# A gated-DeltaNet block on Trainium2: context blocks of both directions inverted in one pass on GpSimd, latent forward blocks on VectorE between the first merges, and the output projection in one stage

## The chip, the cores and the metric

The program runs on one core of a Trainium2 chip. A core has a matrix engine (TensorE, PE in the rows, its weight loads PEld), a vector engine (VectorE, DVE), a scalar engine (ScalarE, ACT), a general engine (GpSimd, POOL), a queue engine that issues DMAs (SyncE, SP), and 16 DMA engines. The metric is the device time of the whole program in microseconds (us); lower is better.

## The reference, cut to what matters

Two blocks run one after the other: a first block (bidirectional gated DeltaNet mixer, then a mixture of experts) and a second block of attention layers. All is float32. The change touches only the mixer's recurrence and its output projection. There are 8 heads of width 128, 256 context tokens and 512 latent tokens; each direction scans its context from a zero state and then its latent tokens from the state left.

```python
def chunk_gated_delta(q, k, v, g, beta, s0):
    a_low = jnp.where(strict, jnp.einsum('bhnid,bhnjd->bhnij', k_beta, k) * decay, 0.0)
    lmat = a_low + jnp.eye(CHUNK, dtype=f32)
    sol = lax.linalg.triangular_solve(lmat, rhs, left_side=True, lower=True, unit_diagonal=True)
    ...
def gdn_out(o, z, o_gain, w_out):
    o = o * lax.rsqrt(jnp.mean(o * o, axis=-1, keepdims=True) + RMS_EPS) * o_gain.astype(jnp.float32) * jax.nn.silu(zf)
    return o.reshape(B, T, H * DV).astype(z.dtype) @ w_out
```

## The kernel before, in words

The recurrence (`gdn_recurrence`, L919) works on token tiles of 128: two context tiles (CT) and four latent ones (LT). For each tile, each half of the heads (4 heads) and each direction there is one "piece", 24 in all: PE makes Gram products and sums of gates, ACT the decays (L1270), DVE the strictly triangular matrix A (`a_piece`, L1376) and, for latent tiles, the attention part (`att_piece`, L1383). SP stores both in DRAM (L991, L995); 4 buffers hold A and 3 hold the attention part, so DVE waits when a store is late.

The solve is by an explicit inverse. The 32x32 diagonal blocks are gathered back from DRAM with one block on each partition (L1004; runs of 128 bytes): 64 partitions for a direction's context, 128 for a direction's latent part. `BlockInverse` (L889) inverts all of them at once by 31 rows, numbered 0 to 30; each row is two dependent tensor operations, a product (L911) and a subtraction (L912), whose sizes grow from 31 to 256 elements and shrink again. `turn` (L916) then copies the transpose. SP writes inverse and transpose to DRAM (L1010, L1011) and reads them as block-diagonal tiles, with off-diagonal parts of A (L1031 to L1034).

Then come merges, numbered y = 4g + c, with g the step (a tile in each direction) and c the direction and half: `product32` (L1112) and `merge32` (L1121, L1124) on PE with `keep32` on ACT between them, DVE's `merged(y)` (`t_early` L1390, `w_full` L1393), then `product64` (L1133), `keep64`, `merge64` (L1143), `fill64` (L1288). `product32(y)` waits for `fill64(y-1)`. Merges 0 to 2 run alone ahead of the main loop, the others between the state updates. Merge 3 is ahead of step 0's solves.

Who inverts what: DVE the forward context blocks after all its pieces; GpSimd the backward context blocks, then the latent forward, then the latent backward ones. Each engine runs its instructions in the order written, and each waits only on semaphores.

`gdn_output` (L1471) normalises the output O (DVE L1520), transposes it on PE (L1544), multiplies by gain and SiLU(z) on DVE (L1526), and in a second block of code, `add_product` (L1556), multiplies by the output weights in float32 on PE (L1579: 64 products of 128x512, two records each), scales by a gate and adds the residual on DVE (L1597, L1599). Each block of code ends with all engines meeting. Elsewhere the kernel already multiplies with split operands: a high part rounded to float32r and a low remainder, three products in place of one (`split_product`, L117; `take_low`, L113).

## Time and profile before

| | us |
|---|---|
| median of 3 runs | 2742.77 (2737.44 to 2743.57) |
| the profiled execution's own time | 2743.18 |
| its span | 2741.4 |
| pieces (PE starts 400.2, DVE's last ends 466.9) | 67 |
| no PE work, DVE and POOL invert blocks | 467 to 516 |
| merges 0 to 3, then main loop | 516 to 737 |
| `gdn_output` with `add_product` | 739.0 to 817.2 |
| experts and second block after that | to the end |

| engine | busy us | share of the span |
|---|---|---|
| PE | 2335.7 | 85% |
| DVE | 1005.3 | 37% |
| ACT | 577.4 | 21% |
| POOL | 264.3 | 10% |

The engine shares are averages over stages that have different limits; the stage from 467 to 516 has none of PE's work in it. The chain of work that ended last, as the page prints it, covers only the last stage, so the chain through the recurrence was followed through the timelines of single engines.

### The profile page before, as it was taken

What the parts mean: (1) busy time and instruction counts of PE and PEld (TensorE: products, weight loads), DVE (VectorE), ACT (ScalarE), POOL (GpSimd) and SP (SyncE); (2) the same over time, 40 slices, a digit from 0 to 9 for tenths busy, and PEclk for the clock granted to TensorE, in tenths of its full rate; (3) what the DMA queues carried; (4) which work ended last, traced back from release to release, by engine and by line L of the source; (5) the groups of instructions that cost most, each with busy time, mean ns of one, the idle gap of its engine ahead of it and who ended that gap; (6) DMA issues with size and microseconds to landing.
All of it is one profiled execution on the core that took longest, in us unless ns stands there. A gap on an engine that the chain in (4) does not pass through costs nothing. (4 is left out here: it accounts for less than half of the span.)

```text
span 2741.4 us, 29858 instructions
## 1 busy us (share of the span) xinstructions
PE 2335.7 (85%) x11740; PEld 1512.8 (55%) x11740; DVE 1005.3 (37%) x1774; ACT 577.4 (21%) x1217; POOL 264.3 (10%) x355
## 2 busy tenths in 40 slices
PE   4999986389886888888888888875998989799998
PEld 2877666389835333333333333332775767687776
DVE  3677426335625101101010110104653554464443
ACT  4442213044401100000000000002222421223311
POOL 4233335800000000000000000000000000000000
PEclk8999988599996899999999999997998999899999
DMA  6124627144311799999999999994321022221030
GB/s 215 58 83 134 219 92 203 36 136 119 131 47 61 295 417 417 418 418 417 416 416 417 418 417 418 418 416 156 128 89 34 31 100 77 98 92 62 31 131 31
DMA packets 209191, 569.88 MB, mean 208 GB/s; under 512 B 62553, under 2 KB 97346, under 8 KB 175682
## 3 DMA queue, kind: packets, MB, share of 16 engines
q1 hardware_dynamic: 206296, 559.97, 53.8%
q0 software_dynamic: 2496, 8.40, 1.0%
q8 instruction: 68, 1.11, 0.2%
...
## 5 line engine op out<-in xcount | busy, mean ns | idle before, releaser
L1871 PE MATMUL ps_gate_up<-expert_ring_early,one_expert_columns 128*64 128x512 f32 x512 | 256.8, 660 | 87.7 <-DMA expert_ring_early<-in_moe_w_up_dram 73.9
L1871 PE MATMUL ps_gate_up<-expert_ring,one_expert_columns 128*64 128x512 f32 x512 | 235.3, 614 | 43.7 <-DMA expert_ring<-in_moe_w_up_dram 43.6
L1938 DVE TENSOR_TENSOR hidden_tokens<-silu_gate,ps_gate_up 64x512 f32<-64x512 f32 x64 | 42.4, 690 | 613.2 <-ACT silu_gate L1917 612.6
L1872 PE MATMUL ps_gate_up<-expert_ring_early,one_expert_columns 128*64 128x512 f32 x512 | 257.5, 661 | 0.0
L1872 PE MATMUL ps_gate_up<-expert_ring,one_expert_columns 128*64 128x512 f32 x512 | 236.0, 616 | 0.0
L1852 PE MATMUL ps_down<-expert_ring,hidden_columns 128*64 128x512 f32 x512 | 226.6, 595 | 0.0
L1851 PE MATMUL ps_down<-expert_ring,hidden_columns 128*64 128x512 f32 x512 | 226.6, 595 | 0.0
L1871 PEld LDWEIGHTS ps_gate_up<-expert_ring_early,one_expert_columns 128*64 128x64 f32 x512 | 74.8, 152 | 254.0 <-issue 254.0
L1871 PEld LDWEIGHTS ps_gate_up<-expert_ring,one_expert_columns 128*64 128x64 f32 x512 | 70.4, 141 | 190.5 <-issue 190.5
L1851 PEld LDWEIGHTS ps_down<-expert_ring,hidden_columns 128*64 128x64 f32 x512 | 67.5, 137 | 130.1 <-issue 127.9
L846 DVE SCALAR_TENSOR_TENSOR conv_out<-conv_in,tap_columns,conv_out 128x770 f32<-128x770 f32 (+1 forms) x96 | 122.3, 1274 | 3.4
L120 PE MATMUL even_bank<-stream_high,columns_high 128*128 128x512 f32 x256 | 108.8, 425 | 2.7 <-DVE columns_low L2440 2.7
L114 DVE TENSOR_TENSOR stream_low<-stream_raw,stream_high 128x2048 fp32r<-128x2048 f32 x48 | 110.0, 2292 | 1.6
L120 PE MATMUL odd_bank<-stream_high,columns_high 128*128 128x512 f32 x256 | 107.1, 418 | 2.8 <-DVE columns_low L2440 2.8
L110 DVE CAST stream_high<-stream_raw 128x2048 fp32r<-128x2048 f32 x48 | 58.6, 1221 | 137.3 <-PE out_bank L122 51.9
L120 PE MATMUL ps_lat<-u_columns_high,w_in_high 128*128 128x512 f32 x256 | 107.8, 421 | 0.0
L1917 ACT ACTIVATE silu_gate<-ps_gate_up 64x512 f32<-64x512 f32 x64 | 37.1, 588 | 330.5 <-PE ps_gate_up L1872 330.4
L611 POOL TENSOR_TENSOR w_in_low<-win_ring,w_in_high 128x1024 fp32r<-128x1024 f32 x32 | 84.3, 2634 | 217.9 <-ACT w_in_high L741 217.9
L121 PE MATMUL ps_lat<-u_columns_low,w_in_high 128*128 128x512 f32 x256 | 104.2, 407 | 0.0
L122 PE MATMUL ps_lat<-u_columns_high,w_in_low 128*128 128x512 f32 x256 | 104.1, 407 | 0.0
L121 PE MATMUL even_bank<-stream_low,columns_high 128*128 128x512 f32 x256 | 103.1, 403 | 0.0
L122 PE MATMUL even_bank<-stream_high,columns_low 128*128 128x512 f32 x256 | 103.0, 402 | 0.0
...
## 6 DMA issues: line engine op xcount, KB each, us to landing
...
```

The source lines that it names most:

```text
L110: return nc.vector.tensor_copy(high.bitcast(F32R), x)
L114: return nc.vector.tensor_tensor(low.bitcast(F32R), x, high, ALU.subtract)
L120: nc.tensor.matmul(out, sh, mh, start=start, stop=False)
L121: nc.tensor.matmul(out, sh, ml, start=False, stop=False)
L122: return nc.tensor.matmul(out, sl, mh, start=False, stop=stop)
L611: nc.gpsimd.tensor_tensor(wl[:, n % 2].bitcast(F32R), raw(n), wh[:, n % 2], ALU.subtract).then_inc(low, 1)
L846: ins = nc.vector.scalar_tensor_tensor(out=cv[:, n % 2, a:b], in0=pad[:, n % 2, a + j:b + j], scalar=tap(j), in1=cv[:, n % 2, a:b], op0=AL ...
L1851: mm(psD[LO, e], hT[:, f], dn[n % RING][:, r, 0:COLS], start=(f == 0), stop=(f == FC - 1))
L1852: last = mm(psD[HI, e], hT[:, f], dn[n % RING][:, r, COLS:D], start=(f == 0), stop=(f == FC - 1))
L1871: mm(psA[LO, c], xe[:, e, k], gu[s0][:, j, cols], start=(k == 0), stop=(k == KC - 1))
L1872: last = mm(psA[HI, c], xe[:, e, k], gu[s1][:, j, cols], start=(k == 0), stop=(k == KC - 1))
L1938: nc.vector.tensor_tensor(hid[HI, c % 2], sg[HI, c % 2], psA[HI, c], ALU.mult).then_inc(hidden, 1)
```

## The change

- The context gathers of both directions move from SP to ACT's queue, after the tenth decay. The backward direction's blocks land in `El[0]`, a buffer of the latent inversion, and GpSimd turns them (a transposing copy) into the upper half of `Ec`. A backward triangle turned is a forward one, so one pass of 31 rows on 128 partitions, on GpSimd, inverts both directions; the stores swap inverse and transpose for the backward half.
- GpSimd then inverts the latent backward blocks only. DVE inverts the latent forward blocks after its pieces, with merges 0, 1 and 2 after rows 14, 23 and 30.
- SP stores all 24 pieces without a break; the context gathers and the first loads of k and v no longer stand between the stores of the 8 context and the 16 latent pieces. Those loads now follow the first inputs.
- `gdn_output` and `add_product` become one block of code. The weights are split in four pieces by ACT (high) and GpSimd (low), the columns by ACT and DVE, and the product is 192 float32r products instead of 64 float32 ones. The residual is loaded after the last transpose.

```diff
-                def blocks(u, d, upto):
+                def blocks(d):
                     for i in range(AB):
-                        sp.wait_ge(a_stored[i], 16 * len(range(i, upto, AB)))
-                    E, t0, t1 = (Ec, 0, CT) if u == 0 else (El[d], CT, NT)
-                    n = (t1 - t0) * HEADS
+                        sp.wait_ge(a_stored[i], 16 * len(range(i, len(PIECES), AB)))
+                    if d == 0:
+                        sp.wait_ge(ctx_turned, 1)
+                    n = LT * HEADS
                     for b in range(BLOCKS):
-                        p0 = (d * UNIT_P[0] if u == 0 else 0) + b * n
-                        sp.dma_start(E[p0:p0 + n], A_dram[d][span(b), t0:t1, :, span(b)].rearrange("j t h i -> (t h) j i")).then_inc(e_loaded[u, d], 16)
+                        src = A_dram[d][span(b), CT:NT, :, span(b)].rearrange("j t h i -> (t h) j i")
+                        sp.dma_start(El[d][b * n:(b + 1) * n], src).then_inc(e_loaded[1, d], 16)
...
-                    E, X = (Ec, Xc) if u == 0 else (El[d], Xl[d])
-                    part = slice(d * UNIT_P[0], (d + 1) * UNIT_P[0]) if u == 0 else slice(0, P)
-                    sp.wait_ge(inverted[u, d], 1)
-                    sp.dma_start(W_dram[u][d], X[part].rearrange("p a b -> p (a b)")).then_inc(scattered[u, d], 16)
-                    sp.dma_start(T_dram[u][d], E[part].rearrange("p a b -> p (a b)")).then_inc(scattered[u, d], 16)
+                    if u == 0:
+                        part = slice(d * UNIT_P[0], (d + 1) * UNIT_P[0])
+                        W, T = (Xc[part], Ec[part]) if d == 0 else (Ec[part], Xc[part])
+                        sp.wait_ge(inverted[0, 0], 1)
+                    else:
+                        W, T = Xl[d][:, :, :], El[d][:, :, :]
+                        sp.wait_ge(inverted[1, d], 1)
...
-                store(range(0, LAT0))
+                store(range(0, len(PIECES)))
                 for d in DIRS:
-                    blocks(0, d, LAT0)
+                    blocks(d)
+                for d in DIRS:
+                    scatter(0, d)
+                for d in DIRS:
+                    inputs(0, d)
                 for d in DIRS:
                     load_v(0, d)
                     load_k(0, d)
-                store(range(LAT0, len(PIECES)))
-                for d in DIRS:
-                    blocks(1, d, len(PIECES))
-                scatter(0, 0)
-                inputs(0, 0)
-                scatter(0, 1)
-                inputs(0, 1)
...
-                for i in range(len(PIECES)):
+                for i in range(LAT0 + 2):
+                    decay(i)
+                for i in range(AB):
+                    act.wait_ge(a_stored[i], 16 * len(range(i, LAT0, AB)))
+                for d, E, p0 in ((0, Ec, 0), (1, El[0], UNIT_P[0])):
+                    for b in range(BLOCKS):
+                        src = A_dram[d][span(b), 0:CT, :, span(b)].rearrange("j t h i -> (t h) j i")
+                        act.dma_start(E[p0 + b * CT * HEADS:p0 + (b + 1) * CT * HEADS], src).then_inc(e_loaded[0, d], 16)
+                for i in range(LAT0 + 2, len(PIECES)):
...
-                h1 = slice(UNIT_P[0], 2 * UNIT_P[0])
-                for u, d, inv in ((0, 1, BlockInverse(Ec[h1], Xc[h1], tmp[1][h1], True)),
-                                  (1, 0, BlockInverse(El[0][:, :, :], Xl[0][:, :, :], tmp[1][:, :], False)),
-                                  (1, 1, BlockInverse(El[1][:, :, :], Xl[1][:, :, :], tmp[1][:, :], True))):
-                    inv.clear(nc.gpsimd, seq)
-                    if u == 0:
-                        seq(nc.gpsimd.memset(O, 0.0))
-                    pool.wait_ge(e_loaded[u, d], 16 * BLOCKS)
-                    for j in range(ROWS):
-                        inv.row(nc.gpsimd, seq, j)
-                    inv.turn(nc.gpsimd).then_inc(inverted[u, d], 1)
-                    pool.wait_ge(inverted[u, d], 1)
+                back = slice(UNIT_P[0], 2 * UNIT_P[0])
+                ctx_inv = BlockInverse(Ec[:, :, :], Xc[:, :, :], tmp[1][:, :], False)
+                lat_inv = BlockInverse(El[1][:, :, :], Xl[1][:, :, :], tmp[1][:, :], True)
+                ctx_inv.clear(nc.gpsimd, seq)
+                seq(nc.gpsimd.memset(O, 0.0))
+                lat_inv.clear(nc.gpsimd, seq)
+                for d in DIRS:
+                    pool.wait_ge(e_loaded[0, d], 16 * BLOCKS)
+                nc.gpsimd.tensor_copy(Ec[back], El[0][back].rearrange("p a b -> p b a")).then_inc(ctx_turned, 1)
+                pool.wait_ge(ctx_turned, 1)
+                for j in range(ROWS):
+                    ctx_inv.row(nc.gpsimd, seq, j)
+                ctx_inv.turn(nc.gpsimd).then_inc(inverted[0, 0], 1)
+                pool.wait_ge(inverted[0, 0], 1)
+                pool.wait_ge(e_loaded[1, 1], 16 * BLOCKS)
+                for j in range(ROWS):
+                    lat_inv.row(nc.gpsimd, seq, j)
+                lat_inv.turn(nc.gpsimd).then_inc(inverted[1, 1], 1)
...
-                h0 = slice(0, UNIT_P[0])
-                ctx_inv = BlockInverse(Ec[h0], Xc[h0], tmp[0][h0], False)
+                lat_inv = BlockInverse(El[0][:, :, :], Xl[0][:, :, :], tmp[0][:, :], False)
+                MERGED_AFTER = {14: 0, 23: 1, 30: 2}
...
-                ctx_inv.clear(nc.vector, seq)
+                lat_inv.clear(nc.vector, seq)
                 for i in range(len(PIECES)):
                     piece(i)
-                dve.wait_ge(e_loaded[0, 0], 16 * BLOCKS)
+                dve.wait_ge(e_loaded[1, 0], 16 * BLOCKS)
                 for j in range(ROWS):
-                    ctx_inv.row(nc.vector, seq, j)
-                ctx_inv.turn(nc.vector).then_inc(inverted[0, 0], 1)
-                merged(0)
-                merged(1)
-                merged(2)
+                    lat_inv.row(nc.vector, seq, j)
+                    if j in MERGED_AFTER:
+                        merged(MERGED_AFTER[j])
+                lat_inv.turn(nc.vector).then_inc(inverted[1, 0], 1)
...
+                for i in range(HALVES):
+                    c = i // 2 * COLS
+                    sp.dma_start(raw[:, i], w[:, i % 2 * HK:(i % 2 + 1) * HK, c:c + COLS]).then_inc(w_loaded[i], 16)
+                    if i == 0:
+                        sp.dma_start(szT[:, :, :], z_dram).then_inc(z_loaded, 16)
+                sp.wait_ge(turned, HEADS)
+                sp.dma_start(h[:, :, :], residual).then_inc(h_loaded, 16)
...
+                def weights_high(i):
+                    act.wait_ge(w_loaded[i], 16)
+                    nc.scalar.activation(wh[:, i].bitcast(F32R), raw[:, i], ACT.Copy).then_inc(w_high, 1)
...
+                weights_high(0)
+                weights_high(1)
+                keep_row(0, "gate_mix")
+                for k in range(HEADS):
+                    act.wait_ge(kept, k + 1)
+                    nc.scalar.activation(sh[:, k].bitcast(F32R), szT[:, k], ACT.Copy).then_inc(s_high, 1)
+                weights_high(2)
+                weights_high(3)
+                keep_row(1, "gate_ffn")
...
+                for i in range(HALVES):
+                    pool.wait_ge(w_high, i + 1)
+                    nc.gpsimd.tensor_tensor(wl[:, i].bitcast(F32R), raw[:, i], wh[:, i], ALU.subtract).then_inc(w_low, 1)
...
-                for h in range(HEADS):
-                    dve.wait_ge(turned, h + 1)
-
-                    nc.vector.scalar_tensor_tensor(out=szT[:, h], in0=ps[:, h % 2], scalar=gain, in1=szT[:, h],
-                                                   op0=ALU.mult, op1=ALU.mult).then_inc(kept, 1)
+                for k in range(HEADS + 1):
+                    if k < HEADS:
+                        dve.wait_ge(turned, k + 1)
+
+                        nc.vector.scalar_tensor_tensor(out=szT[:, k], in0=ps[:, k % 2], scalar=gain, in1=szT[:, k],
+                                                       op0=ALU.mult, op1=ALU.mult).then_inc(kept, 1)
+                    if k:
+                        dve.wait_ge(s_high, k)
+                        take_low(nc, sl[:, k - 1], szT[:, k - 1], sh[:, k - 1]).then_inc(s_low, 1)
+                dve.wait_ge(h_loaded, 16)
+                dve.wait_ge(row_kept, 1)
...
-        add_product(nc, "gdn_w_out", per, szT, wt, gate=per["gate_mix"],
-                    residual=dram["x"].rearrange("b (t p) d -> p (b t) d", p=P))
+                pe.wait_ge(row_kept, 1)
+                rows(1, 5)
+                for n in range(2 * LT):
+                    i, t = n // LT, n % LT
+                    if i:
+                        pe.wait_ge(taken, t + 1)
+                    for k in range(KC):
+                        if t == 0 and k % HK == 0:
+                            pe.wait_ge(w_low, 2 * i + k // HK + 1)
+                        if n == 0:
+                            pe.wait_ge(s_low, k + 1)
+                        half = 2 * i + k // HK
+                        last = split_product(nc, psD[:, t], [x[:, k, t * P:(t + 1) * P] for x in (sh, sl)],
+                                             [x[:, half, k % HK] for x in (wh, wl)], k == 0, k == KC - 1)
+                    last.then_inc(done, 1)
...
-            recycle(nc)
-            gdn_output(nc, dram, per, O, z_dram)
+        recycle(nc)
+        gdn_output(nc, dram, per, O, z_dram)
```

**ACT** in the row of decays, just where the latent pieces begin. Before:

```order
L1270 ACTIVATE decay<-gdn_bank,token_scalars 128x128 [waits a_ready,rowsums]
L1270 ACTIVATE decay<-gdn_bank,token_scalars 128x128 x3
L1270 ACTIVATE decay<-gdn_bank,token_scalars 128x128 [waits a_ready,rowsums]
L1270 ACTIVATE decay<-gdn_bank,token_scalars 128x128 x3
L1270 ACTIVATE decay<-gdn_bank,token_scalars 128x128 [waits a_ready,rowsums]
```

Now:

```order
L1272 ACTIVATE decay<-gdn_bank,token_scalars 128x128 [waits a_ready,rowsums]
L1272 ACTIVATE decay<-gdn_bank,token_scalars 128x128 x3
L1314 DMA blocks_ctx<-a_turned 16x32x32 [waits a_stored2,a_stored3,a_stored1,a_stored0]
L1314 DMA blocks_ctx<-a_turned 16x32x32 x3
L1314 DMA blocks_lat<-a_turned 16x32x32 x4
L1272 ACTIVATE decay<-gdn_bank,token_scalars 128x128 [waits att_ready,a_ready,rowsums]
L1272 ACTIVATE decay<-gdn_bank,token_scalars 128x128 x3
```

Eight gathers, with a wait for the stores of the first 8 pieces, now stand between two decays.

**DVE** at the end of the inversion and the first merges. Before, all 31 rows on the context blocks stand ahead of the turn and of merge 0:

```order
L911 TENSOR_TENSOR row_update<-blocks_ctx,inverse_ctx 64x31 [waits row_chain0]
L912 TENSOR_TENSOR inverse_ctx<-inverse_ctx,row_update 64x31 [waits row_chain0]
L916 COPY blocks_ctx<-inverse_ctx 64x1024 [waits row_chain0]
L1390 TENSOR_TENSOR t_early<-t_diagonal,gdn_bank 64x256 [waits x1_done]
L1393 TENSOR_TENSOR w_full<-w_diagonal,gdn_bank 128x512 [waits x2_done]
```

Now, around merge 0 (row 14 is the one on 255 elements):

```order
L911 TENSOR_TENSOR row_update<-blocks_lat,inverse_lat 128x255 [waits row_chain0]
L912 TENSOR_TENSOR inverse_lat<-inverse_lat,row_update 128x15x17 [waits row_chain0]
L1406 TENSOR_TENSOR t_early<-t_diagonal,gdn_bank 64x256 [waits x1_done,row_chain0]
L1409 TENSOR_TENSOR w_full<-w_diagonal,gdn_bank 128x512 [waits x2_done]
L911 TENSOR_TENSOR row_update<-blocks_lat,inverse_lat 128x256
L912 TENSOR_TENSOR inverse_lat<-inverse_lat,row_update 128x16x16 [waits row_chain0]
```

The same two instructions of a merge stand again after the row of 192 elements (row 23) and after the last. DVE's rows are now on the latent blocks and on both sides of a merge.

**SP** where the inverse of the context leaves. Before, each direction is stored and read by itself:

```order
L1010 DMA w_blocks<-inverse_ctx 64x1024 [waits inverted00]
L1011 DMA t_blocks<-blocks_ctx 64x1024
L1031 DMA t_diagonal<-t_blocks 32x8x32 [waits diagonals_zeroed,scattered00]
L1031 DMA t_diagonal<-t_blocks 32x8x32 x3
L1031 DMA w_diagonal<-w_blocks 32x8x32 x4
L1033 DMA a_off_0<-a_turned 32x8x32 x2
```

Now:

```order
L1015 DMA w_blocks<-inverse_ctx 64x1024 [waits inverted00]
L1016 DMA t_blocks<-blocks_ctx 64x1024
L1015 DMA w_blocks<-blocks_ctx 64x1024 [waits inverted00]
L1016 DMA t_blocks<-inverse_ctx 64x1024
L1036 DMA t_diagonal<-t_blocks 32x8x32 [waits diagonals_zeroed,scattered00]
```

Both directions wait for the same semaphore, GpSimd's, and both stores stand ahead of the first read.

## Rows read from the trace of the kernel before

**Rows 1.** Windows: us, busy (x) of PE, PEld, DVE, ACT, POOL, PEclk, DMA share, GB/s.

```profile
423.00:431.00 8.00, 8.00 (x75) 8.00 (x73) 5.87 (x19) 3.84 (x15) 0.00 (x0) 1.00 1.02 119
446.00:466.00 20.00, 17.57 (x158) 17.38 (x156) 15.03 (x46) 10.03 (x36) 17.65 (x31) 0.98 0.59 221
467.00:516.00 49.00, 0.00 (x0) 0.00 (x0) 35.12 (x62) 0.00 (x0) 40.09 (x70) 0.50 0.35 56
```

**Rows 2.** Timelines of ACT, SP, POOL: context gathers (start us, us, engine line op).

```profile
422.87 1.15 ACT L1270 ACTIVATE decay<-gdn_bank,token_scalars 128x128 f32<-128x128 f32 x4 [0.20 <-PE gdn_bank L1103]
...
422.87 4.02 SPq L1004 DMA_DIRECT2D blocks_ctx<-a_turned  x8
...
431.01 0.25 POOL L911 TENSOR_TENSOR row_update<-blocks_ctx,inverse_ctx 64x31 f32<-64x31 f32 x1 [20.40 <-DMA blocks_ctx<-a_turned]
...
468.04 1.89 POOL L916 COPY blocks_ctx<-inverse_ctx 64x1024 f32<-64x1024 f32 x1
```

**Rows 3.** Timelines of DVE: its last piece, then the forward context inversion.

```profile
466.17 0.68 DVE L1383 TENSOR_TENSOR att_piece<-gdn_bank,decay 128x512 f32<-128x512 f32 x1
...
480.04 0.56 DVE L911 TENSOR_TENSOR row_update<-blocks_ctx,inverse_ctx 64x256 f32<-64x256 f32 x1
...
492.63 0.67 DVE L911 TENSOR_TENSOR row_update<-blocks_ctx,inverse_ctx 64x175 f32<-64x175 f32 x1
...
502.75 1.46 DVE L916 COPY blocks_ctx<-inverse_ctx 64x1024 f32<-64x1024 f32 x1
```

**Rows 4.** Timelines of SP and PE: inverse stored, then the first merge product.

```profile
504.24 0.53 SPq L1010 DMA_DIRECT2D w_blocks<-inverse_ctx  x1
...
516.24 2.07 PE L1112 MATMUL gdn_bank<-t_diagonal,a_off 128*128 128x128 f32 x8 [52.67 <-DMA a_off<-a_turned]
```

**Rows 5.** Timeline of DVE: merges 0, 2 and 3 ahead of the main loop.

```profile
520.14 0.41 DVE L1390 TENSOR_TENSOR t_early<-t_diagonal,gdn_bank 64x256 f32<-64x256 f32 x1 [15.93 <-PE gdn_bank L1121]
...
522.15 0.69 DVE L1393 TENSOR_TENSOR w_full<-w_diagonal,gdn_bank 128x512 f32<-128x512 f32 x1 [1.59 <-PE gdn_bank L1124]
...
538.20 0.42 DVE L1390 TENSOR_TENSOR t_early<-t_diagonal,gdn_bank 64x256 f32<-64x256 f32 x1 [6.34 <-PE gdn_bank L1121]
...
547.22 0.42 DVE L1390 TENSOR_TENSOR t_early<-t_diagonal,gdn_bank 64x256 f32<-64x256 f32 x1 [6.33 <-PE gdn_bank L1121]
```

**Rows 6.** Timelines of POOL and DVE: rows side by side, and the copy.

```profile
474.83 0.38 POOL L911 TENSOR_TENSOR row_update<-blocks_lat,inverse_lat 128x31 f32<-128x31 f32 x1 [3.67 <-DMA blocks_lat<-a_turned]
...
501.34 0.60 POOL L911 TENSOR_TENSOR row_update<-blocks_lat,inverse_lat 128x231 f32<-128x231 f32 x1
...
501.37 0.64 DVE L911 TENSOR_TENSOR row_update<-blocks_ctx,inverse_ctx 64x31 f32<-64x31 f32 x1
...
514.01 1.91 POOL L916 COPY blocks_lat<-inverse_lat 128x1024 f32<-128x1024 f32 x1
```

**Rows 7.** Timelines of DVE and SP: the stall among pieces, the latent gathers.

```profile
438.37 0.69 DVE L1383 TENSOR_TENSOR att_piece<-gdn_bank,decay 128x512 f32<-128x512 f32 x1 [8.39 <-DMA attention<-att_piece]
...
468.95 5.99 SPq L1004 DMA_DIRECT2D blocks_lat<-a_turned  x8
```

**Rows 8.** Timelines of DVE and PE in the output stage.

```profile
745.58 4.63 DVE L1520 TENSOR_TENSOR residual<-residual,o_ss 128x1024 f32<-128x1024 f32 x4
...
751.49 6.02 DVE L1526 SCALAR_TENSOR_TENSOR silu_z_again<-o_ps,vector_columns,silu_z_again 128x512 f32<-128x512 f32 x8 [1.28 <-PE o_ps L1544]
...
758.88 56.87 PE L1579 MATMUL gdn_w_out_ps<-gdn_w_out_pieces,silu_z_again 128*128 128x512 f32 x128 [2.15 <-PEq L1488]
...
816.50 0.69 DVE L1599 TENSOR_TENSOR residual<-residual,gdn_w_out_tmp 128x512 f32<-128x512 f32 x1
```

**Rows 9.** Timeline of PE in the second block, and the page's group of L611.

```profile
2152.78 0.40 PE L120 MATMUL even_bank<-stream_high,columns_high 128*128 128x512 f32 x1
...
2154.16 0.39 PE L120 MATMUL even_bank<-stream_high,columns_high 128*128 128x512 f32 x1
...
L611 POOL TENSOR_TENSOR w_in_low<-win_ring,w_in_high 128x1024 fp32r<-128x1024 f32 x32 | 84.3, 2634 | 217.9 <-ACT w_in_high L741 217.9
```

102 lines of the change are left out of this document (37 added, 65 removed).

## The prediction

> **What bounds the kernel now.** I read the windows first. From 467 to 516 us PE does nothing, its granted clock is 0.50, and DVE and GpSimd are busy for 35 and 40 of the 49 us [rows 1]. Next, DVE's timeline: its last piece ends at 466.9, the 31 inversion rows of the forward context blocks follow without a gap, the turn ends at 504.2 [rows 3]. SP then stores the inverse, and PE's first merge product comes at 516.24, after 52.67 us of idleness [rows 4]. So the stage's end is set by DVE inverting after its pieces, though GpSimd had inverted the other direction by 469.9 [rows 2]. Then merges 0 to 3 run one after the other, 9.0 us each: DVE's `t_early` stands at 520.14, 538.20 and 547.22 for merges 0, 2 and 3 [rows 5]. The output stage is bound by PE: 56.87 us of float32 products [rows 8].
>
> **The new chain into the merges.** I place everything on the clock of the old trace.
>
> *Gathers.* ACT ends its tenth decay at 424.0; eight issues took SP 4.0 us, so they end at 428.0; the last landed 4.1 us after its issue (426.9 to 431.0) [rows 2], so 432.1. But now SP's stores run beside them. Stores alone keep the DMA engines at 0.59, gathers alone at 1.02 [rows 1]. If the shares simply add, the gathers get 0.41 of the engines and their 8.1 us become 19.8, 11.7 us more. The latent gathers speak against that: twice the bytes (256 blocks against 128) were issued in 6.0 us [rows 7], so the context's need at most some 3 us of the engines' capacity, and 3/0.41 is 7.3, no delay. I take 2 us (0 to 11.7), nearer to the second row since it is of the same kind of transfer: 434.1. The Trainium skill (DMA: Bandwidth & Descriptors, Queues, rings and completion order) says that a DMA engine takes turns between queues packet by packet; by it neither queue starves, which would put the delay in the lower half, and no row here shows two queues at once.
>
> *One pass for both directions.* First the turning copy, 1.9 us like GpSimd's copy of the same size [rows 2]: 436.0. The pass has 128 partitions. On 64 it took 37.0 us (431.01 to 468.04) [rows 2], on 128, beside DVE's rows, 39.2 (474.83 to 514.01) [rows 6]; so partitions cost nothing, and most of the new pass runs beside the pieces. I take 37.8: 473.8, with the copy 475.7. The store began at 504.24 before [rows 4]; it is 28.5 us earlier. From store to first product 12.0 us passed [rows 4]; the second direction's store lies in the wait for the first to land. So the first product is at 487.7, merge 0's `t_early` 3.9 us on, at 491.6, and its `w_full` ends 6.6 us on, at 494.3 [rows 4, 5].
>
> *The pieces.* DVE waited 8.39 us for an attention store that stood in SP's queue behind gathers and the loads of k and v [rows 7]. These are gone from there; eight issues on ACT delay two decays by some 2 us, which PE's lead hides but for under 1. Pieces end near 459. Latent gathers and landing took 8.0 us (466.85 to 474.83) [rows 3, 6], so DVE's rows start at 467. This gain is worth nothing: rows 0 to 14 took 13.3 us, to 480.04 [rows 3], and even at 20 us, beside GpSimd, end before 491.6. If the stall stays, its 8 us only just use up this slack.
>
> *Rows between merges.* This is what is late next. At the end of the old pass the two engines' rows run in step: GpSimd's operation on 231 elements starts at 501.34 and takes 0.60, DVE's on 31 elements starts at 501.37 and takes 0.64 [rows 6]. A small DVE row costs what GpSimd's large one costs. In the new kernel GpSimd is in its latent pass from 475.7 to 516.8 all the while. Rows 15 to 23 took 12.6 us (480.04 to 492.63) [rows 3] with GpSimd in rows of like size; they start at 494.3, after merge 0, and end at 506.9. PE would have had merge 1 ready at 500.6 (491.6 + 9.0), so it waits 6.3. Merge 1 is 1.1 us of DVE (0.41 + 0.69) [rows 5]: 508.0. Rows 24 to 30 took 10.1 (492.63 to 502.75) [rows 3] beside GpSimd's largest rows; now it is in its last ones and its copy. I take 8.6 (4 to 10.1): merge 2's `t_early` at 516.6 instead of 538.20, 21.6 earlier. PE's other products of merge 2 are done by then, so the wait of 1.59 behind `t_early` [rows 5] goes: merge 3 is 23.1 us earlier, at 524.1. DVE's turn (1.5 us) ends near 519, GpSimd's pass at 516.8; both latent inverses are there before the main loop begins and are first used in its third step. The first k and v loads move behind the first inputs and have over 20 us. The loop itself is unchanged.
>
> **The output stage.** Now DVE's four normalising operations (4.63 us) are followed by eight of scaling (6.02), and PE starts its product at 758.88, 1.4 us after them, a block boundary that goes [rows 8]. Added ahead of the product: eight `take_low` on DVE at 0.69, as for the same size in the last row, 5.5 us [rows 8]. GpSimd subtracts four pieces of 128x2048; half that size takes 2.63 [rows 9], so 5.3 each. By the row in step [rows 6], a DVE operation with both inputs in SBUF waits until GpSimd's ends: the first subtraction then holds up normalising by 5 us (0 to 5.3), the second the first `take_low` by 1.5 (0 to 5.3, part of it lies in a wait for ACT). The Trainium skill (SBUF — State Buffer, Who interferes with whom) says just this: a VectorE instruction with two SBUF inputs and a GpSimd one that reads SBUF exclude each other for a whole instruction, and PE never waits; the trace agrees where it has such a pair, 0.64 for 31 elements. By that rule the stage gains next to nothing; were there no such lock it would gain 6.5 us more. ACT's four weight copies have no row; between nothing and 2.9 (twice DVE's 1.46 for half the elements [rows 3]), I take 2 and call them hidden under loads and DVE. The loads are the same 6 MB, which before had landed when PE began. The second gate row on PE, at most 4.1 us (twice 2.07 for half the products [rows 4]), lies under DVE's last columns. So the product starts 5.5 + 5 + 1.5 - 1.4 = 10.6 us later. Three float32r products take 0.69 us (six starts in 1.38) [rows 9], 192 take 44.2, and I add 1 for the low clock at the start: 45.2 against 56.87, 11.7 less. Net 1.1 us gained (7.6 gained to 3 lost).
>
> **Sum.** 2743.2 (the profiled execution's own time) - 23.1 - 1.1 = 2719.0. The median of the runs is 0.4 below that execution; I stay at 2719. What follows the stage (experts, second block) starts by its own barriers and shifts as a whole: the expert loads are issued after this stage, not at a fixed time.
>
> **Rivals.**
> 1. *No lock, or a lighter one.* DVE's rows at their own pace never hold a merge: merge 3's `t_early` at 491.6 + 27.1 = 518.7, 28.5 gained, and the output stage 7.6: 2707 (2713 if only the rows are free). For it: merges with an input in PSUM took 0.41 and 0.69 throughout, with GpSimd at work or not. Against it: the rows in step [rows 6]. 0.14.
> 2. *Gathers slowed by stores*, the full 11.7 us: GpSimd's pass, the first product and the rows behind it all move by 9.7: 2729. For it the shares that add to over 1 [rows 1], against it the faster latent gathers [rows 7]. 0.15.
> 3. *Slower: the lock goes to GpSimd twice for each DVE operation.* In the old pass DVE got in after each one. If it gets in after every second, the 16 rows behind merge 0 pay 32 times 0.65, 20.8 us, row 14 ends some 3.4 us after merge 0 is ready, and merge 3 is 1.1 us later than before; with the output's 3 lost: 2747. It decides from the point where a DVE row operation beside GpSimd takes over some 1.3 us. Against it: 0.64 in the trace. 0.04.
> 4. *The gain is given back later*, in the expert stage, which waits for its loads; it would need loads issued at a fixed time, and they are not. 2742. 0.04.
>
> **How the numbers follow.** The forecast has 0.58, with its own range 2713 to 2725 (rows 24 to 30 at either end, gathers at 0 to 4). The remaining 0.05 are mixtures of rivals 1 and 2 with it, inside the range. From 2707 to 2731 (rival 2 with rows 24 to 30 at 10.1) about 0.9 lie; the unknown costs need that width. A difference under 0.2%, 5.5 us, cannot be told from no change. Faster: forecast, rivals 1 and 2 and mixtures, 0.93 with what such a sum leaves out; same 0.03 (most of rival 4); slower 0.04.
>
> **What would show it.** Right: GpSimd's first row near 436 and one pass of 37 to 39 us; PE's first merge product near 488 instead of 516; DVE idle ahead of merge 0 and PE waiting for DVE ahead of merges 1 and 2; merge 3's `t_early` 23 us earlier; the main loop (547 to 737) as long as before; `take_low` or normalising operations of 5 us beside GpSimd; the output product 45 us, starting 30 us into its stage. Wrong: context gathers landing after 438, DVE rows of 128x31 at 0.2 us beside GpSimd, or a main loop that waits for a latent inverse.

## The result

Over the first comparison the changed kernel took 2703.49 us (median of 4 runs, 2697.10 to 2709.14) against 2743.17 us (4 runs, 2737.44 to 2743.85): a ratio of 0.9859 with a 95% interval of 0.9832 to 0.9886. That is 39.7 us less, where 24.2 had been predicted, and 3.5 us under the low end of the range. The direction and the mechanism in the recurrence came out as forecast, the size did not. Two more comparisons of the same pair, made among the experiments below, gave 0.9891 (0.9863 to 0.9919) and 0.9883 (0.9864 to 0.9903). The medians of all runs, 52 of the kernel before and 15 of the changed one, are 2738.0 and 2705.7, 32.3 us apart. So some 7 us of the first difference did not repeat.

In the changed kernel L911 and L912 are still the rows of an inversion, L916 the turn; L1406 is `t_early` (L1390 before), L1570 the normalising (L1520 before) and L120 to L122 are the three products of a split product. Timelines have the start in us, the duration in us, engine, line and operation, tiles written and read, and in brackets the idle time before and what ended it.

The windows of the changed kernel (PE, PEld, DVE, ACT, POOL busy; then PE's granted clock, share of the DMA engines, GB/s), against [rows 1]:

```profile
466.00:485.00 19.00, 0.31 (x1) 0.32 (x2) 14.60 (x29) 0.00 (x0) 16.43 (x34) 0.50 0.53 95
485.00:521.00 36.00, 25.05 (x137) 21.61 (x137) 23.59 (x40) 4.66 (x10) 24.47 (x41) 0.50 0.31 82
```

PE now idles for 19 us where it had idled for 49. The chain that ends this gap, on GpSimd, SP and PE (against [rows 2, 4]):

```profile
431.04 1.99 POOL L1367 COPY blocks_ctx<-blocks_lat 64x1024 f32<-64x1024 f32 x1 [20.15 <-DMA blocks_lat<-a_turned]
470.19 1.89 POOL L916 COPY blocks_ctx<-inverse_ctx 128x1024 f32<-128x1024 f32 x1
472.11 0.53 SPq L1015 DMA_DIRECT2D w_blocks<-inverse_ctx  x1
484.69 2.08 PE L1114 MATMUL gdn_bank<-t_diagonal,a_off 128*128 128x128 f32 x8 [30.64 <-DMA a_off<-a_turned]
504.71 1.11 PE L1135 MATMUL gdn_bank<-t_early,a_off 64*64 64x64 f32 x8 [5.12 <-DVE t_early L1406]
```

The turning copy starts at 431.04 (434.1 was predicted), the one pass for both directions takes 37.0 us, and the first product comes at 484.69 (487.7). The last line is the new wait that was predicted: PE stands 5.12 us for merge 1's `t_early`, because DVE is still at its rows. DVE itself, against [rows 5]:

```profile
488.67 0.41 DVE L1406 TENSOR_TENSOR t_early<-t_diagonal,gdn_bank 64x256 f32<-64x256 f32 x1 [7.10 <-PE gdn_bank L1123]
493.34 0.78 DVE L912 TENSOR_TENSOR inverse_lat<-inverse_lat,row_update 128x255 f32<-128x255 f32 x1
504.25 0.41 DVE L1406 TENSOR_TENSOR t_early<-t_diagonal,gdn_bank 64x256 f32<-64x256 f32 x1
510.70 1.96 DVE L912 TENSOR_TENSOR inverse_lat<-inverse_lat,row_update 128x31 f32<-128x31 f32 x1
520.88 0.42 DVE L1406 TENSOR_TENSOR t_early<-t_diagonal,gdn_bank 64x256 f32<-64x256 f32 x1 [5.39 <-PE gdn_bank L1123]
```

Merge 0 comes at 488.67, after 7.10 us in which DVE did nothing, merge 1 at 504.25, 15.6 later instead of 9.0, merge 3 at 520.88, 26.3 us earlier than in [rows 5]. The line at 510.70 shows a row operation of 31 elements that takes 1.96 us: GpSimd's turn of 1.93 us starts at 510.66. The prediction had named a row of 31 elements at 0.2 us beside GpSimd as a sign against it, and there is one: the subtraction at 465.85 takes 0.19. It begins together with GpSimd's operation on 135 elements, and this one then takes 0.51 instead of the 0.42 of the same operation at 436.30. So it is not always DVE that waits.

The output stage, DVE, GpSimd and PE (against [rows 8]):

```profile
716.94 8.93 DVE L1570 TENSOR_TENSOR residual<-residual,o_ss 128x1024 f32<-128x1024 f32 x4
728.60 2.21 DVE L114 TENSOR_TENSOR o_columns_low<-silu_z_again,o_columns_high 128x512 fp32r<-128x512 f32 x1
737.70 1.47 DVE L114 TENSOR_TENSOR o_columns_low<-silu_z_again,o_columns_high 128x512 fp32r<-128x512 f32 x2
718.40 5.25 POOL L1560 TENSOR_TENSOR gdn_w_out_low<-gdn_w_out_raw,gdn_w_out_high 128x2048 fp32r<-128x2048 f32 x1 [7.47 <-ACT gdn_w_out_high L1531]
736.21 2.61 PE L1599 MATMUL ps_row<-identity_and_ones,mod_columns 128*128 128x128 f32 x16
738.58 0.47 PE L120 MATMUL gdn_w_out_ps<-gdn_w_out_high,o_columns_high 128*128 128x512 f32 x1
```

Normalising takes 8.93 instead of 4.63 and the first `take_low` 2.21 instead of 0.69, both beside a GpSimd subtraction. PE's product starts at 738.58, while DVE's last low parts are still being made, and ahead of it stands the second gate row. DVE's last addition ends at 783.83, and with it the stage's work.

### The profile page after: what moved, and what is told of

Its sections match the earlier page's. It is cut to its first block and busy times, and to the rows that moved or that the text cites. A ratio compares the mean times of both kernels' runs of the same rounds, so it can differ in the third digit from the quotient of the medians.

```text
span 2699.5 us, 29938 instructions
## 1 busy us (share of the span) xinstructions
PE 2307.3 (85%) x11804; PEld 1514.6 (56%) x11804; DVE 1019.7 (38%) x1782; ACT 589.6 (22%) x1229; POOL 249.5 (9%) x295
## 5 line engine op out<-in xcount | busy, mean ns | idle before, releaser
L1897 PE MATMUL ps_gate_up<-expert_ring_early,one_expert_columns 128*64 128x512 f32 x512 | 252.0, 650 | 87.6 <-DMA expert_ring_early<-in_moe_w_up_dram 73.8
L1898 PE MATMUL ps_gate_up<-expert_ring_early,one_expert_columns 128*64 128x512 f32 x512 | 252.8, 651 | 0.0
L120 PE MATMUL even_bank<-stream_high,columns_high 128*128 128x512 f32 x256 | 107.7, 421 | 2.8 <-DVE columns_low L2466 2.8
L120 PE MATMUL odd_bank<-stream_high,columns_high 128*128 128x512 f32 x256 | 107.0, 418 | 2.8 <-DVE columns_low L2466 2.8
L120 PE MATMUL ps_lat<-u_columns_high,w_in_high 128*128 128x512 f32 x256 | 108.0, 422 | 0.0
L611 POOL TENSOR_TENSOR w_in_low<-win_ring,w_in_high 128x1024 fp32r<-128x1024 f32 x32 | 84.3, 2636 | 217.9 <-ACT w_in_high L741 217.9
L122 PE MATMUL ps_lat<-u_columns_high,w_in_low 128*128 128x512 f32 x256 | 104.1, 407 | 0.0
L122 PE MATMUL even_bank<-stream_high,columns_low 128*128 128x512 f32 x256 | 102.6, 401 | 0.0
## 6 DMA issues: line engine op xcount, KB each, us to landing
expert_ring<-in_moe_w_up_dram SPq DMA_DIRECT2D x32, 2048.0 KB, 24.2
```

The source lines that it names most:

```text
L120: nc.tensor.matmul(out, sh, mh, start=start, stop=False)
L122: return nc.tensor.matmul(out, sl, mh, start=False, stop=stop)
L611: nc.gpsimd.tensor_tensor(wl[:, n % 2].bitcast(F32R), raw(n), wh[:, n % 2], ALU.subtract).then_inc(low, 1)
L1897: mm(psA[LO, c], xe[:, e, k], gu[s0][:, j, cols], start=(k == 0), stop=(k == KC - 1))
L1898: last = mm(psA[HI, c], xe[:, e, k], gu[s1][:, j, cols], start=(k == 0), stop=(k == KC - 1))
```

## Where the time went, stage by stage

One cut serves for all the profiles: A, from the first decay on ACT behind 400 us to merge 3's `t_early`; B, from there to the end of the last state update; C, the output stage, to the issue of the router's weights; D, the router stage, to the clearing of the experts' total; E, the experts, from the first accumulation to the last gated output; F, from there to the last residual addition of the second block. "Rise" is how long behind the start of B the granted clock of PE goes from 0.50 to 1.00. All worked out from starts in the timelines, in us.

```
                    A     rise    B      C      D      E      F
before            141.9   13.7  190.2   81.0   90.5   863.0  838.9
before, again     140.8    8.6  188.2   81.3   90.5   860.3  838.6
output only       140.2    9.3  188.1   76.6   86.8   860.0  837.6
recurrence only   116.4    8.7  188.0   80.6   89.5   860.2  834.5
changed           116.6    8.5  187.9   76.3   86.5   860.1  837.7
changed, second   115.9    9.2  188.3   76.5   86.5   860.0  837.6
changed, third    114.7   14.2  190.7   77.8   90.4   863.0  839.0
```

The first profiled execution of each kernel, "before" and "changed", differ by 41.9 us at their last operation. A is 25.3 of these, C 4.7 and the start of the first decay 1.0; B, D, E and F bring 10.4 more (the rest is rounding and a step between D and E), and a third profile of the very same changed kernel (last line) has given all of these back. So they can't be put down to the change; in B and D they go with the stretches in which the clock stands at 1.2 or 2.4 GHz (below), for E and F no row shows why. In D one thing stays open. In the four profiles with the old output stage D was 89.5 to 90.5; in the twelve with a new one, those of the experiments below among them, it was 86.5 to 86.8 seven times and 90.2 to 90.5 five times. The new output stage may make the short D possible, which on average would be worth some 2 us; so few profiles don't show it. The mean of A is 141.0 in three profiles without the new recurrence and 115.9 in the four with it, C is 81.0 in three with the old output stage and 76.8 in four with the new one: 25.1 and 4.2, 29.3 us of the change that the stages show.

## The experiments

**Each part alone, and the whole again.** One kernel has the new recurrence with the old `gdn_output` and `add_product`, the other the old recurrence with the new `gdn_output`; the functions are taken over word for word.

> The changed kernel once more, beside the kernel before and the two kernels that do one part each. Theory (the gain is 28.6 us in the recurrence, 4.7 in the output stage, 3.1 in the router stage and the rest, 5.5, in expert and second-block stages by chance of the run): the median comes to 2743 - 36.4 = 2706.5, within the spread of 2697 to 2709, and the stages up to the first expert matmul repeat to 1 us (merge 3's t_early 320 to 321 after 200 us, that is near 520.9; end of the recurrence near 708.5; first expert matmul near 876), while the 3.2 us between the first and the last expert do not repeat. Rival (the change does something to the expert stage): the expert stage is again 3 us shorter than in the kernel before and the median is again near 2703.

> The recurrence part of the change alone; output stage as before. Theory: merge 3's t_early at 520.9, the main loop (t_early of merge 3 to the end of the recurrence) 2.3 us shorter than before because the granted clock of PE rises some 6 us earlier in it, the recurrence ends 28.6 us earlier; then the float32 product and a router stage whose 64 small matmuls take 12.5 us as before. Total 2743 - 28.6 = 2714.5. Rival (router and experts gain from the recurrence part): total 2703 + 4.7 = 2708, and router matmuls near 10.1 us.

> The output stage of the change alone; recurrence as before. Theory: stage 4.7 us shorter (73.5 against 78.2), then the 64 router matmuls 10.1 us instead of 12.5 and the transposes ahead of them 0.8 us shorter, because the granted clock of PE, higher after the float32r product, falls later; total 2743 - 4.7 - 3.1 = 2735. Rival (the clock in the router stage is chance, or comes from the recurrence): router matmuls 12.5 us, total 2738.5.

Measured, beside 17 runs of before with median 2737.47: the whole 2705.89 (6 runs), the recurrence alone 2710.74 (6 runs, ratio 0.9904, 0.9879 to 0.9930), the output stage alone 2727.26 (12 runs, 0.9965, 0.9945 to 0.9986). The whole repeats in A to C (its starts are 3.5 to 4 us later, since its first decay is 4.1 later), and its median is the forecast one. The 3 us of the expert stage, which had been called chance of the changed kernel, repeated too (E 860.0). The totals expected were counted from 2743, while the kernel before took 2737.47 here; so the differences are what compares. The recurrence alone, with A and B of the changed kernel, takes 26.7 us less where 28.6 were expected. The output stage alone takes 10.2 less where 7.8 were expected; its profile has C 4.4 and D 3.7 shorter than the first of before. The theory that the output part alone decides the router stage's 86.5 us fitted these profiles and fell later: with the same output stage D took 90.4 in the changed kernel's third profile and in the kernel with moved rows. The two parts add up to 36.9 us where the whole has 31.6, which such medians leave open (5.5 us from run to run).

So the kernel before was profiled again:

> The kernel before once more, for a second profile. Theory (part of the 41.9 us between the two profiled executions is chance of the first profile of before): the expert stage, from its first to its last accumulation, takes 858.8 us as in every other kernel and not 861.8; the loop from merge 3's t_early to the end of the recurrence takes 187 us, not 189.05, where the granted clock rises earlier; the router stage (from its weight load to the first memset of the experts) stays at 89.5 to 90.5 us, against 86.5 in kernels with the new output stage. Rival (before's stages really are longer): 861.8, 189.0 and 90.5 repeat.

One run, 2740.20 us. In the table above (whose cuts B and E are 1.1 and 1.2 us longer than those of the expectations) B fell to 188.2 with a rise at 8.6, E to 860.3, and D stayed at 90.5: what the first profile of before had more in B and E did not repeat, as the theory says. It is one profile.

**Is it GpSimd that makes DVE's rows long?** GpSimd begins its latent pass only behind DVE's:

```diff
                 pool.wait_ge(e_loaded[1, 1], 16 * BLOCKS)
+                pool.wait_ge(inverted[1, 0], 1)
                 for j in range(ROWS):
```

> As the changed kernel, but GpSimd begins its latent pass only when DVE has ended its own (one wait more; the pass then runs from about 508 to 547 beside the main loop, whose third step uses it). Theory (a DVE operation with both inputs in SBUF waits for GpSimd's): without GpSimd rows 0 to 14 take under 10 us instead of 16.3, rows 15 to 23 under 8 instead of 13.0 and rows 24 to 30 under 5, so merge 1 follows merge 0 after 9.0 us instead of 15.6, PE's wait of 5.12 ahead of merge 1 goes, and merge 3's t_early stands at 515.8 instead of 520.9; total 5 us less than the changed kernel, unless the loop's DVE operations now wait for GpSimd or its third step for the inverse (it would be 0 to 8 more). Rival (the rows cost that much by themselves): rows 15 to 23 take 12 to 13 us again and merge 3 stays at 520.9.

DVE in this kernel, for the rows beside those shown above:

```profile
491.70 0.41 DVE L1407 TENSOR_TENSOR t_early<-t_diagonal,gdn_bank 64x256 f32<-64x256 f32 x1 [9.03 <-PE gdn_bank L1123]
495.61 0.42 DVE L912 TENSOR_TENSOR inverse_lat<-inverse_lat,row_update 128x255 f32<-128x255 f32 x1
502.07 0.41 DVE L1407 TENSOR_TENSOR t_early<-t_diagonal,gdn_bank 64x256 f32<-64x256 f32 x1
518.71 0.42 DVE L1407 TENSOR_TENSOR t_early<-t_diagonal,gdn_bank 64x256 f32<-64x256 f32 x1 [5.39 <-PE gdn_bank L1123]
```

The same subtraction on 128x255 takes 0.42 without GpSimd and 0.78 beside it; rows 15 to 23 take 7.8 us instead of 13.0, merge 1 follows merge 0 after 10.4 instead of 15.6 (9.0 had been expected, but the rows start only behind merge 0's 2.5 us on DVE) and merge 3 after 27.0 instead of 32.2. The lock (a DVE operation with both inputs in SBUF waits until GpSimd's ends) is real and costs 5.2 us here. The Trainium skill (SBUF — State Buffer, Who interferes with whom) says that such a pair of instructions excludes each other for the whole instruction. The changed kernel's trace agrees: 1.96 us for 31 elements beside a copy of 1.93. GpSimd's pass, now beside the main loop, ends at 552.5 and holds nothing up: B is 190.1 with a late rise (14.4), as in the third profile of the changed kernel. The first 15 rows took 13.9, not under 10: until 475.2 GpSimd was still in its context pass. The median is 2699.61 (4 runs; ratio 0.9848, 0.9813 to 0.9883); the 5 us less than the changed kernel are seen in the stage, the ratios' intervals overlap.

**Rows where DVE idles.** If the rows are long, they can be put elsewhere:

```diff
-                MERGED_AFTER = {14: 0, 23: 1, 30: 2}
+                MERGED_AFTER = {18: 0, 22: 1, 28: 2}
```

> As the changed kernel, but DVE takes merges 0, 1 and 2 after rows 18, 22 and 28 instead of 14, 23 and 30. Theory (beside GpSimd a row costs 1.45 us, and rows 15 to 23 hold up merge 1 by 6.6 us while DVE stood idle for 7.1 us ahead of merge 0): rows 15 to 18 go into that idle time (5.8 us), rows 19 to 22 take 5.8, merge 1's t_early comes 9.0 us behind merge 0's and merge 3's 27.1 behind it instead of 32.2; total 5.1 us less than the changed kernel, if the clock in the main loop rises at the same place. Rival (later rows hold merge 2, or the loop waits for the inverse that DVE now ends later): merge 3 gains under 2 us, or the third step starts later by what merge 3 gained.

```profile
496.34 0.41 DVE L1406 TENSOR_TENSOR t_early<-t_diagonal,gdn_bank 64x256 f32<-64x256 f32 x1 [1.05 <-PE gdn_bank L1123]
505.37 0.41 DVE L1406 TENSOR_TENSOR t_early<-t_diagonal,gdn_bank 64x256 f32<-64x256 f32 x1 [0.25 <-PE gdn_bank L1123]
523.35 0.42 DVE L1406 TENSOR_TENSOR t_early<-t_diagonal,gdn_bank 64x256 f32<-64x256 f32 x1 [2.34 <-PE gdn_bank L1123]
```

The idle time of 7.10 ahead of merge 0 is down to 1.05, merge 1 follows after 9.03, merge 3 after 27.01: 5.2 us less between merge 0 and merge 3, as expected, with GpSimd at work all the while. The median is 2698.99 (5 runs; 0.9854, 0.9833 to 0.9874).

**The gathers, and the first loads of k and v.** Two kernels: one issues the context gathers on SP behind the stores of the context pieces, the other puts the four first loads of k and v back to where they stood. The edit of the second:

```diff
-                store(range(0, len(PIECES)))
+                store(range(0, LAT0))
+                for d in DIRS:
+                    load_v(0, d)
+                    load_k(0, d)
+                store(range(LAT0, len(PIECES)))
...
-                for d in DIRS:
-                    load_v(0, d)
-                    load_k(0, d)
```

> As the changed kernel, but the eight context gathers are issued by SP, in its one queue, behind the stores of the context pieces, instead of by ACT. Theory (the gathers were never slowed, and only the slack of the pieces hangs on the queue): GpSimd's turning copy starts where it did, 26.7 us behind the first decay (plus or minus 1); the pieces end some 4 to 8 us later, because stores of attention pieces stand behind the gathers, DVE's first row comes that much later and still ends row 14 ahead of merge 0; merges and total stay within 1 us of the changed kernel. Rival (ACT's own queue is what keeps the gathers fast, beside the stores): the turning copy starts 2 us or more later and all merges move with it.

> As the changed kernel, but the four first loads of k and v go out between the stores of the context pieces and those of the latent pieces on SP, where they stood before the change. Theory (those loads, not the gathers, made the wait of 8.39 us, and the pieces have slack): DVE waits again 6 to 8.4 us for a store of an attention piece, the last piece ends some 61 us behind the first decay instead of 53, DVE's rows start 8 us later, row 14 ends at about merge 0's readiness (2 us before to 2 after); the turning copy stays within 1 us, merge 3 comes 0 to 2 us later and the total within 2 us of the changed kernel. Rival (the queue does not matter, the pieces are faster for another reason): the last piece again ends 52 to 53 us behind the first decay.

With the gathers on SP nothing is later: the turning copy starts 25.6 us behind the first decay (26.7 in the changed kernel), the pieces end 52.2 behind it (53.0), and the median is 2700.89 (4 runs; 0.9864, 0.9843 to 0.9885). The expected 4 to 8 us of stall did not come, so the move of the gathers to ACT's queue bought nothing.

With the loads early the forecast came out in one half. The pieces end at 59.8, which costs nothing by itself, row 14 being done 4.6 us ahead of merge 0. But the turning copy starts 31.3 us behind the first decay, 5.3 later than the mean of 26.0 in four profiles with the new recurrence, and A is 121.2 instead of 115.9. The issues, with KB each and median us from issue to landing, first with the loads early (424 to 440), then in the changed kernel (421 to 440); below them the issuing of the last four gathers (ACTq) and what came of it:

```profile
v_tile<-v_tokens SPq DMA_DIRECT2D x2, 512.0 KB, 5.7
blocks_ctx<-a_turned ACTq DMA_DIRECT2D x4, 64.0 KB, 10.2
blocks_lat<-a_turned ACTq DMA_DIRECT2D x4, 64.0 KB, 4.9
...
432.19 4.57 ACTq L1315 DMA_DIRECT2D blocks_lat<-a_turned  x4
436.88 2.18 ACT L1273 ACTIVATE decay<-gdn_bank,token_scalars 128x128 f32<-128x128 f32 x8 [10.08 <-issue]
438.11 1.13 DVE L1393 SCALAR_TENSOR_TENSOR a_piece<-gdn_bank,token_scalars,decay 128x128 f32<-128x128 f32 x4 [9.21 <-issue]
```

```profile
blocks_ctx<-a_turned ACTq DMA_DIRECT2D x4, 64.0 KB, 3.1
blocks_lat<-a_turned ACTq DMA_DIRECT2D x4, 64.0 KB, 4.4
...
424.13 3.15 ACTq L1314 DMA_DIRECT2D blocks_lat<-a_turned  x4
```

So the gathers are slowed from another queue, but by the 2 MB of k and v, beside which the DMA engines' share is 1.00 from 424 to 436, and not by the stores. The first four land after 10.2 us instead of 3.1. The last four, for which the turning copy waits, land after 4.9 instead of 4.4, but are issued late: the eight issues take ACT 11.0 us (425.80 to 436.76) instead of 5.2. DVE's wait of 9.21 us is not the one that was expected either. It does not stand ahead of an attention part, for a store, but ahead of an A, for a decay, and ACT makes this decay only when its issues are out. The median is 2711.69 (4 runs; 0.9916, 0.9892 to 0.9939), not within 2 us of the changed kernel.

**The loads alone, in the kernel before.** The same four loads moved behind the first inputs, and nothing else:

> The kernel before with one edit: the four first loads of k and v go out on SP behind the first inputs, as in the changed kernel, instead of between the stores of the context and of the latent pieces. Theory (these 2 MB, not the gathers, made DVE's wait of 8.39 us, and before the change DVE's rows follow its pieces without a gap): the last piece ends 52 to 53 us behind the first decay instead of 60 to 61.6, all of the chain behind it moves, merge 3's t_early comes 132 to 134 us behind the first decay instead of 140.8 to 141.9, and the total is 7.5 us less than before (6 to 9). Rival (the gathers alone keep the queue blocked, or the gathers' landing sets the end through GpSimd): under 2 us.

```profile
456.22 0.68 DVE L1383 TENSOR_TENSOR att_piece<-gdn_bank,decay 128x512 f32<-128x512 f32 x1
538.52 0.42 DVE L1390 TENSOR_TENSOR t_early<-t_diagonal,gdn_bank 64x256 f32<-64x256 f32 x1 [6.34 <-PE gdn_bank L1121]
```

Here the wait of 8.39 us ahead of an attention part is down to 1.33, with the gathers still on SP, so it was the loads'. The last piece ends 51.0 us behind the first decay and merge 3 stands at 132.7, 8.3 us earlier than the mean of before; median 2727.34 (5 runs; 0.9948, 0.9935 to 0.9962), 11.8 less than before and more than the 6 to 9 expected. A third of what the recurrence part gained could be had with this move alone. The other 16.8 us of A are left for the single pass on GpSimd and the new place of the rows, which no run separates. That the total gained 11.8 and A only 8.3 is not explained by a stage.

**The output stage.** First the low parts of the first two weight quarters on DVE:

```diff
-                for i in range(HALVES):
+                for i in range(2, HALVES):
                     pool.wait_ge(w_high, i + 1)
...
+                dve.wait_ge(w_high, 1)
+                take_low(nc, wl[:, 0], raw[:, 0], wh[:, 0]).then_inc(w_low, 1)
...
+                    if k == 4:
+                        dve.wait_ge(w_high, 2)
+                        take_low(nc, wl[:, 1], raw[:, 1], wh[:, 1]).then_inc(w_low, 1)
```

> As the changed kernel, but DVE itself takes the low parts of the first two quarters of the output weights (one between normalising and scaling, one behind the fourth column), GpSimd only those of the last two. Theory (a GpSimd subtraction excludes DVE operations with two SBUF inputs): the four normalising operations take 4.63 us again instead of 8.93, the first take_low of the columns 0.67 instead of 2.21, and DVE pays 2 times 2.3 us for the two quarters, one of them under a wait of 1.3; the product starts 26 us into the stage instead of 28.2, gain 2 us (0 to 3). Rival (the 4.3 us were something else, as cold SBUF reads or the loads of the weights): normalising takes 8.9 us again and the product starts 3 us later than in the changed kernel.

```profile
719.50 4.63 DVE L1570 TENSOR_TENSOR residual<-residual,o_ss 128x1024 f32<-128x1024 f32 x4
730.40 0.69 DVE L114 TENSOR_TENSOR o_columns_low<-silu_z_again,o_columns_high 128x512 fp32r<-128x512 f32 x1 [2.75 <-ACT o_columns_high L1548]
727.02 1.91 ACT L1531 ACTIVATE gdn_w_out_high<-gdn_w_out_raw 128x2048 fp32r<-128x2048 f32 x1 [5.73 <-DMA gdn_w_out_raw<-in_gdn_w_out_dram]
```

Normalising is back at 4.63, so the 4.3 us were GpSimd's. The product starts 30.7 us behind the last state update, later than the changed kernel's 29.8 and not 2 us earlier as expected. The stage gained nothing (C 77.6, as the changed kernel's third profile with 77.8; median 2707.32, 6 runs): ACT stands 5.73 us for the load of the second quarter, with the columns queued behind it, and DVE waits 2.75 for them. Under the lock this wait for a load had been hidden. The next kernel takes these waits and the second gate row out of the way of the product: DVE takes the second quarter's low part behind the columns, ACT converts that quarter behind the fifth column, PE makes the second gate row ahead of the transposes. Cut to the order:

```diff
-                weights_high(0)
-                weights_high(1)
                 keep_row(0, "gate_mix")
+                weights_high(0)
                 for k in range(HEADS):
...
+                    if k == 4:
+                        weights_high(1)
...
+                dve.wait_ge(w_high, 1)
+                take_low(nc, wl[:, 0], raw[:, 0], wh[:, 0]).then_inc(w_low, 1)
...
+                dve.wait_ge(w_high, 2)
+                take_low(nc, wl[:, 1], raw[:, 1], wh[:, 1]).then_inc(w_low, 1)
...
                 rows(0, 2)
+                pe.wait_ge(row_kept, 1)
+                rows(1, 5)
                 pe.wait_ge(normed, LT)
```

> As the changed kernel, with another order in the output stage: DVE takes the low parts of the first two weight quarters (one behind normalising, one behind the eighth column), GpSimd those of the last two; ACT converts the second quarter behind the fifth column instead of ahead of the first, where it waited 5.4 to 5.7 us for its load; PE makes the second gate row before the transposes instead of ahead of the product. Theory (normalising held 4.3 us by GpSimd, then ACT's columns held by the second quarter's load, then 2.6 to 3.6 us of the gate row on PE): normalising takes 4.63, no take_low waits 2.75 for ACT, and the product starts 24 to 25.5 us into the stage instead of 28.2; the stage is 3 to 4 us shorter. Rival (the first product waits for loads or for the second quarter's low part anyway): it starts by 25 but stands at its fifth step for 2 us or more, and the stage gains under 1.5.

> Both edits: merges 0, 1, 2 after rows 18, 22, 28, and the new order of the output stage. Theory: they lie in different stages and add up, 5.1 us and 3 to 4 us less than the changed kernel, that is a total of some 2696 to 2698 beside 2705.6 for the changed kernel and 2738.9 for the one before (medians of all their runs). Rival: one of the two is off the path, total 2700 or more.

```profile
735.97 0.78 PE L120 MATMUL gdn_w_out_ps<-gdn_w_out_high,o_columns_high 128*128 128x512 f32 x1
741.90 0.50 PE L120 MATMUL gdn_w_out_ps<-gdn_w_out_high,o_columns_high 128*128 128x512 f32 x1 [1.64 <-DVE gdn_w_out_low L114]
```

These are PE's first and fifth step in the kernel with the new order alone. The product starts 22.4 us behind the last state update instead of 29.8, begins slowly (0.78 for its first matmul instead of 0.47) and waits 1.64 at its fifth step, in which the rival had its part; C is 72.1, 4.2 to 5.7 less than in the profiles of the changed kernel, where 3 to 4 had been expected. In the total this gain is not shown: the median of this kernel, 2704.24 (6 runs, 0.9889, 0.9867 to 0.9911), can't be told from the changed kernel's. With the rows moved too: 2697.55 (5 runs, 0.9856, 0.9833 to 0.9879), at the upper end of what was expected.

**Last comparison**, the changed kernel and the one with both edits on one chip:

> The changed kernel a third time, beside e12_both_again. Theory (the change is worth 24.9 us in the recurrence up to merge 3 and 4.7 in the output stage, and what the first two profiled executions differed by beyond that is the place at which the granted clock rises): 2738 less 29 to 33, that is near 2706; router stage 86.5 or 90.4 us and the stretch from merge 3's t_early to the end of the recurrence 188 or 190 us, one or the other. Rival: the 39.7 us of the first comparison repeat, total near 2699.

> The kernel with both edits (merges after rows 18, 22, 28; new order of the output stage) again, beside the changed kernel. Theory: 5.1 and 4.3 us less in their stages, so 9.4 us less than the changed kernel where the clock's places are alike, near 2697. Rival (a shorter recurrence and output stage make the clock rise later, which gives the gain back): under 4 us less.

2707.73 and 2695.85 (5 runs each), ratios to before 0.9883 (0.9864 to 0.9903) and 0.9837 (0.9823 to 0.9851). Over both of its comparisons the kernel with both edits has a median of 2696.7 (10 runs), 9.0 less than the changed kernel's 2705.7, where 9.4 were expected; beside each other in this comparison the two differ by 11.9. It beats both kernels. Its stages say the same: A 110.8 and 109.8, 5.6 less than 115.9, and C 72.1 and 72.0, 4.7 less than 76.8. The rival, a later clock that gives the gain back, had only the first of its profiles for it (rise 14.2), the second has 8.9. The router stage's 64 matmuls in two profiles of the changed kernel, the third and the first:

```profile
804.13 12.64 PE L1707 MATMUL ps_logits<-w_router,ffn_columns 128*128 128x16 f32 x64 [1.12 <-PEq L444]
```

```profile
798.42 10.14 PE L1707 MATMUL ps_logits<-w_router,ffn_columns 128*128 128x16 f32 x64 [1.12 <-PEq L444]
```

One kernel, 10.14 and 12.64 us. The same holds behind the start of the main loop, third and first profile (windows as above):

```profile
521.00:536.00 15.00, 13.97 (x78) 12.68 (x76) 2.21 (x4) 5.63 (x18) 0.00 (x0) 0.51 0.19 32
```

```profile
530.00:545.00 15.00, 12.25 (x118) 11.15 (x116) 3.50 (x6) 10.34 (x34) 0.00 (x0) 1.00 0.35 90
```

Merge 3's `t_early` stands at 521.6 in the one and 520.9 in the other, 32.2 us behind merge 0 in both, and PE did the same merges before it. The granted clock is 0.51 (1.2 GHz) up to 536 in one and 1.00 (2.4 GHz) from 530 in the other. What decides between the two stays open.

## Why the prediction was too small

Two steps of the sum failed. The output stage was priced at 1.1 us and gave 4.2 to 4.7: its product starts earlier and runs shorter than summed. And the gathers were given 2 us for stores beside them, which cost nothing. The mechanism of the recurrence, with the lock, was right. The terms, one by one:

- *What bounds it, and what is late next:* right. DVE idle ahead of merge 0, PE waiting ahead of merge 1, the rows in step with GpSimd. From merge 0 to merge 3 32.5 us were predicted and 32.2 measured; rows 15 to 23 took 13.0 (12.6 predicted). The sum is closer than its parts, which is luck: rows 24 to 30 took 7.5 instead of 8.6, and from merge 2 to merge 3 8.2 us passed instead of 7.5, since 0.73 of the wait that was to go stayed.
- *The gathers:* the step that took 2 us for stores beside them was wrong. The turning copy stood 3.1 us earlier than forecast, of which 1.0 is the whole execution's earlier start. Beside stores the gathers landed after 3.1 and 4.4 us, in the kernel before after 3.9. The row behind this step was misread: the share of 1.02 "alone" in [rows 1] is taken from 423 to 431, and SP had issued the loads of k and v from 426.93 on; up to 427 the share was 0.71. It was these loads that could have slowed the chain, by 5.3 us, and they had been moved away. The prediction saw the move and gave it no price. For its sum this did no harm, since the chain was built up from the landings of the kernel before; but of the gain that it forecast a part is the move's, 5.3 us of A in the changed kernel, 8.3 in the kernel before. Rival 2 had a mechanism that exists, with the wrong cause.
- *The pass:* 37.0 against 37.8. From its store to the first product 12.6 against 12.0.
- *The recurrence as a whole:* 25.1 (25.3 in the first pair) against 23.1. The lock in it was priced at 5.4 us (28.5 less 23.1 in rival 1), and 5.2 were measured.
- *The output stage:* this is the term that was mis-sized most, 1.1 predicted, 4.2 to 4.7 measured. The lock's two pieces were right (4.3 for 5, 1.5 for 1.5). Wrong was when the product starts, 8.3 us later than before instead of 10.6: DVE was held 0.7 less in normalising, its eight low parts cost 1.0 less than eight times 0.69, and the product starts 0.6 ahead of the end of the last one, its first step needing only the first. The gate row was called hidden and stood for 2.6 us right ahead of the product. From the product's start to the stage's end 45.3 us passed against 58.3 before, 13.1 less instead of 11.7: the products on PE took 43.8 us instead of 45.2, and the low clock at their start, priced at 1 us, hardly showed (0.47 for the first matmul). That the loads have landed in time was wrong too; ACT waited 5.36 us for the second quarter (5.73 in the run above), hidden only under the lock.
- *"What follows shifts as a whole":* not refuted for the kernel (D stays open), wrong for the two executions compared. B, D, E and F were 10.4 us shorter in the first profile of the changed kernel than in the first of before, and as long in its third.
- *The anchor:* the sum was made against 2743.2. Over 52 runs the kernel before has a median of 2738.0. From there the forecast of 24.2 would have said 2713.8; the 15 runs of the changed kernel have 2705.7. So of the 15.5 us by which the first median missed the forecast, 8.1 are the model's; the other 7.4 are scatter (the profiled execution of before lay 5.2 above its median, the first median of the changed kernel 2.2 below).
- *Rival 1:* its 2707 lies nearer to both medians than the forecast, but what it assumes, no lock, is what the runs refute. That it comes close is luck.

Of the 8.1 us, 5.1 are explained by stages (2.0 in the recurrence, 3.1 in the output stage). The rest, 3 us, is not settled: the shorter D may have some 2 of them, and it is no more than medians of this size leave open.
